# Sparse and stick-breaking attention heads taken in pairs, in a fused block kernel on one core

## The reference, cut to what matters

```python
# even layer: 8 query heads of 64, 2 key/value heads, indexer of 4 heads, 64 keys kept per query
q, k, v, qi, ki, wi, u = split(h @ w_in)                 # q and k are RMS-normed per head
score = (relu(qi @ ki.T) * wi).sum(heads) * IDX_SCALE    # causal
_, sel = top_k(score, 64)
attn = softmax(q @ k[sel].T * 64 ** -0.5) @ v[sel]
pooled = multiscale_pool(u) @ pool_w * pool_scale        # 4 groups of 128
x = x + concat([attn, pooled]) @ w_out                   # 1024 x 1024
# odd layer: 16 heads of 64
z = q @ k.T * 64 ** -0.5
brk = where(s < t, softplus(z), 0)
a = where(s < t, exp(log_sigmoid(z) - sum_of_later(brk)), 0)
x = x + (a @ v) @ w_out
```

## Time and profile before

| what | value |
|---|---|
| three runs | 1335.97, 1337.49, 1373.87 us; median 1337.49 |
| profiled execution | 1334.04 us, its span 1332.3 us |
| mean granted clock of PE in it | 0.977 of full speed |
| busy: PE, DVE, ACT, POOL | 1245.0 (93%), 785.6 (59%), 613.4 (46%), 107.6 us (8%) |
| DMA moved | 219.94 MB, 164 GB/s read |

### The profile page before, as it was taken

How to read it: one execution, slowest core, us unless ns; L and a number is a source line. 1 busy time by engine, 2 the same in 40 slices (tenths; PEclk the granted TensorE clock), 3 DMA queues, 4 the chain that set the end, 5 groups by cost and what they waited for, 6 DMA issues and landing times.

```text
span 1332.3 us, 21042 instructions
## 1 busy us (share of the span) xinstructions
PE 1245.0 (93%) x8609; PEld 1139.1 (85%) x8609; DVE 785.6 (59%) x1245; ACT 613.4 (46%) x950; POOL 107.6 (8%) x172
## 2 busy tenths in 40 slices
PE   2899999998989899999998699999999999899998
PEld 2889989876789899887888479999989887899997
DVE  7888987654595354555546756555554433655554
ACT  2557623433455354554444335434453654544442
POOL 0200000031030000112100410000000133000000
PEclk9999999999999999999989589999999999999999
DMA  9896779402557465322522054555545322555552
GB/s 328 293 307 190 253 249 313 165 1 85 184 175 215 124 213 165 124 91 69 170 92 72 32 177 141 190 189 189 190 158 171 114 96 76 176 173 183 186 189 95
DMA packets 164880, 219.94 MB, mean 165 GB/s; under 512 B 5868, under 2 KB 135696, under 8 KB 164784
## 3 DMA queue, kind: packets, MB, share of 16 engines
q1 hardware_dynamic: 163984, 216.82, 50.3%
q0 software_dynamic: 800, 1.77, 0.4%
HBM read 217.53 MB, written 1.05 MB: 164 GB/s over the span
## 4 chain that ended last, share of the span: by engine, by line
PE 74%; DVE 12%; DMA 6%; ACT 6%; issue 2%; SPq 0%; ACTq 0%; DVEq 0%
PE ps L646 12%; PE ps L650 11%; PE ps L647 11%; PE ps L709 5%; PE ps L714 5%; PE ps L710 5%; DMA raw_weights<-in_a_w_in 4%; DVE w_lo L1592 4%; PE ps L687 3%; PE ps L682 3%; PE ps L683 3%; DVE acc L1674 2%; ACT w_hi L1271 1%; PE ps L962 1%; PE ps L907 1%
## 5 line engine op out<-in xcount | busy, mean ns | idle before, releaser
L1592 DVE TENSOR_TENSOR w_lo<-raw_weights,w_hi 128x1024 fp32r<-128x1024 f32 x348 | 423.7, 1228 | 282.3 <-ACT w_hi L1271 280.7
L1271 ACT ACTIVATE w_hi<-raw_weights 128x1024 fp32r<-128x1024 f32 x348 | 362.8, 1054 | 415.5 <-PE ps L714 110.6
L646 PE MATMUL ps<-act_hi,w_hi 128*128 128x256 f32 x1616 | 405.6, 289 | 3.8 <-ACT w_hi L1271 3.8
L647 PE MATMUL ps<-act_lo,w_hi 128*128 128x256 f32 x1616 | 397.4, 283 | 0.0
L646 PEld LDWEIGHTS ps<-act_hi,w_hi 128*128 128x128 f32 x1616 | 310.4, 192 | 12.1 <-issue 8.5
L647 PEld LDWEIGHTS ps<-act_lo,w_hi 128*128 128x128 f32 x1616 | 310.7, 192 | 3.3 <-issue 2.4
L650 PE MATMUL ps<-act_hi,w_lo 128*128 128x256 f32 x1616 | 228.0, 284 | 7.1 <-DVE w_lo L1592 7.1
L650 PEld LDWEIGHTS ps<-act_hi,w_lo 128*128 128x128 f32 x1616 | 209.2, 193 | 8.0 <-DVE w_lo L1592 7.9
L709 PE MATMUL ps<-w_hi,act_hi 128*128 128x512 f32 x320 | 126.7, 396 | 2.5 <-DVE work L1777 1.9
L710 PE MATMUL ps<-w_hi,act_lo 128*128 128x512 f32 x320 | 125.4, 392 | 0.0
L714 PE MATMUL ps<-w_lo,act_hi 128*128 128x512 f32 x320 | 86.9, 392 | 0.0
(11 more groups left out here) (258 smaller groups left out, 1421.4 us busy)
## 6 DMA issues: line engine op xcount, KB each, us to landing
raw_weights<-in_ffn_w SPq DMA_DIRECT2D x66, 1024.0 KB, 5.2
raw_weights<-in_a_w_in SPq DMA_DIRECT2D x32, 1024.0 KB, 6.1
raw_weights<-in_mod_w SPq DMA_DIRECT2D x24, 1024.0 KB, 5.9
raw_weights<-in_kv_w SPq DMA_DIRECT2D x16, 1024.0 KB, 5.6
raw_weights<-in_b_w_in SPq DMA_DIRECT2D x16, 1024.0 KB, 5.4
raw_weights<-in_od_w_qkv SPq DMA_DIRECT2D x12, 1024.0 KB, 5.2
raw_weights<-in_kv_mod_w SPq DMA_DIRECT2D x8, 1024.0 KB, 5.8
raw_weights<-in_a_w_out SPq DMA_DIRECT2D x8, 1024.0 KB, 5.0
```

What stands on the lines that cost most here:

```text
L646: pe.matmul(dst, wh[:, k, :], act_hi[:, base + k, :], start=(k == 0), stop=False)
L647: pe.matmul(dst, wh[:, k, :], act_lo[:, base + k, :], start=False, stop=False)
L1271: act.activation(half_view(w_hi, s), HALVES[s][2], ACT.Copy).then_inc(hi_done, 1)
L1592: dve.tensor_tensor(half_view(w_lo, s), HALVES[s][2], half_view(w_hi, s).bitcast(F32), ALU.subtract).then_inc(lo_done, 1)
```

## The change

- **Sparse section, order of weights:** `ev_u`, `ev_q`, `ev_kv` in place of `ev_kv`, `ev_q`, `ev_u`; output chunks pooled first (4, 5, 6, 7, then 0 to 3). The pooling matmuls come before the heads, the scale of the pooled result moves from DVE to ACT.
- **Sparse section, heads:** four pairs instead of eight single heads. Two heads' matmuls stand one behind the other on different halves of the array's rows (logits) or columns (values) and in different PSUM banks. The output chunks stand between the steps of the pairs. ACT, not DVE, copies the outputs. DVE's splits stand at other rounds of the selection.
- **Stick-breaking section:** eight pairs in ten steps with two halves each. DVE writes the breaks twice, as fp32 and rounded to fp32r; POOL subtracts the two; the break matmuls run on both parts as fp32r, 6 per head instead of 3 of fp32. The two `affine_select` per head go; an fp32r matmul of the identity by a matrix with a large negative number adds the mask to z.
- **Constants:** the identity's 128 KB come by POOL's queue instead of SP's; the masks come as two transfers.
- **Banks:** the even layer's output sum moves to banks 0 to 3, which the projections use.

```diff
@@ -64,9 +64,9 @@
             pieces.append(("mod", *mods.pop(0)))
     pieces += [("forget", 0)] + [("b_in", n) for n in (*range(8, 16), *range(8))]
     pieces += [("b_out", n) for n in range(8)]
-    pieces += [("ev_qi", 0), ("ev_small", 0), ("ev_kv", 0), ("ev_q", 0), ("ev_q", 1), ("ev_u", 0), ("ev_u", 1),
+    pieces += [("ev_qi", 0), ("ev_small", 0), ("ev_u", 0), ("ev_u", 1), ("ev_q", 0), ("ev_q", 1), ("ev_kv", 0),
                ("pool_w", 0)]
-    pieces += [("ev_out", n) for n in range(4)]
+    pieces += [("ev_out", n) for n in (2, 3, 0, 1)]
...
@@ -103,11 +103,12 @@
     add("q", "v" * 8)
     add("norm2", "vvvv")
     add("ev_i", "aa")
+    add("ev_u", "aa")
+    add("ev_q0", "v")
+    add("ev_q1", "v")
     add("ev_k", "v")
     add("ev_v", "a")
-    add("ev_q", "vv")
-    add("ev_u", "aa")
-    add("ev_pool", "vv")
+    add("ev_pool", "aa")
     add("norm3", "vvvv")
     add("up0", "v" * FC)
...
@@ -216,7 +223,7 @@
 
         def y_bank(j, t, n):
 
-            return ps[:, (0 if j in (1, 4) else 4) + 2 * t + n, :]
+            return ps[:, (0 if j in (1, 2, 4) else 4) + 2 * t + n, :]
...
@@ -489,6 +507,7 @@
 
         @block.gpsimd
         def _(pool):
...
+            pool.wait_ge(st("ds_split"), HE // 2)
+            pool.tensor_scalar(far_r, causal[:, 0:P], -1.0, FAR, ALU.is_ge, ALU.mult).then_inc(st("sb_far"), 1)
+            for p in range(HO // 2 + 2):
+                if p < HO // 2:
+                    for h in (2 * p, 2 * p + 1):
+                        pool.wait_ge(st("sb_soft"), h + 1)
+                        pool.tensor_tensor(sb_brk_lo[h % 2], sb_brk[h % 2], sb_brk_hi[h % 2].bitcast(F32), ALU.subtract)\
+                            .then_inc(st("sb_lo"), 1)
+                if 1 <= p <= HO // 2:
+                    c = p - 1
                     split_output(c, o_full[:, c % 2, :], st("sb_out"), st("sb_split"), OUT2 + c)
 
         down_half = {}
...
+                for t in range(NT):
+                    for e, rows in enumerate(pair_rows):
+                        ins = pe.matmul(ds_bank(p, e)[:, P * t:P * t + P * (t + 1)], evq[rows, p, t * P:(t + 1) * P],
+                                        evk[rows, p // 2, 0:P * (t + 1)], start=True, stop=True)
+                ins.then_inc(st("ds_logits"), 1)
+
+            def ds_turn(p):
+                pe.wait_ge(st("ds_prob"), p + 1)
+                for e in range(2):
+                    for b in range(3):
+                        blk = slice(b * P, (b + 1) * P)
+                        ins = pe.transpose(ds_bank(p, e)[:, blk], ds_prob[:, p % 2, e, blk], ident)
+                ins.then_inc(st("ds_turned"), 1)
+
...
+                for e, rows in enumerate(pair_rows):
+                    pe.matmul(ds_bank(p, e)[rows, 0:T], v[0], ds_probT[:, e, 0:T], start=True, stop=False)
+                for e, rows in enumerate(pair_rows):
+                    ins = pe.matmul(ds_bank(p, e)[rows, P:T], v[1], ds_probT[:, e, T:S3], start=False, stop=True)
+                ins.then_inc(st("ds_o"), 1)
+
+            def ev_out_chunk(c):
+                if c == 4:
+                    pe.wait_ge(unit_free["a"], before("a", unit[0] - 1))
+                    pe.wait_ge(unit_free["v"], before("v", unit[0] - 1))
+                if c >= 4:
+                    pe.wait_ge(st("ev_pooled"), (c - 4) // 2 + 1)
+                else:
+                    pe.wait_ge(st("ds_split"), c + 1)
+                out_half("ev_out", OUT2 + c, c == 4, c == 3)
...
+            ds_logits(0)
+            ev_out_chunk(4)
+            ds_logits(1)
+            ev_out_chunk(5)
+            ds_turn(0)
+            ev_out_chunk(6)
+            ds_pv(0)
+            ds_turn(1)
+            ds_logits(2)
+            ev_out_chunk(7)
+            ds_pv(1)
+            ds_logits(3)
+            ev_out_chunk(0)
+            ds_turn(2)
+            ev_out_chunk(1)
+            ds_pv(2)
+            ds_turn(3)
+            ev_out_chunk(2)
+            ds_pv(3)
+            ev_out_chunk(3)
...
+                for bank, _ in pair:
+                    pe.matmul(diagonal_blocks(bank[:, 0:S3]), ident_r,
+                              far_r.rearrange("p (b t) -> p b t", b=1).to_broadcast([P, 2, P]),
+                              start=True, stop=False, skip_group_check=True)
+                for bank, rows in pair:
+                    pe.matmul(bank[:, 0:T], odk[rows, p, 0:P], odq[rows, p, :], start=False, stop=False,
+                              skip_group_check=True)
+                for bank, rows in pair:
+                    ins = pe.matmul(bank[:, T:S3], odk[rows, p, P:T], odq[rows, p, P:T], start=False, stop=False,
+                                    skip_group_check=True)
+                ins.then_inc(st("sb_z"), 1)
+
+            def minus_breaks(p):
+
+                for h in (2 * p, 2 * p + 1):
+                    bank = sb_bank(h)
+                    pe.wait_ge(st("sb_lo"), h + 1)
+                    for b in (sb_brk_hi[h % 2], sb_brk_lo[h % 2]):
+                        pe.matmul(bank[:, 0:T], neg_after_r, b[:, 0:T], start=False, stop=False, skip_group_check=True)
+                        pe.matmul(bank[:, P:T], neg_ones_r, b[:, T:S3], start=False, stop=False, skip_group_check=True)
+                        ins = pe.matmul(bank[:, T:S3], neg_after_r, b[:, T:S3], start=False,
+                                        stop=(b is sb_brk_lo[h % 2]), skip_group_check=True)
+                    ins.then_inc(st("sb_log"), 1)
...
+            pe.wait_ge(x_done, 16)
+            pe.wait_ge(st("sb_far"), 1)
+            od_bank = [None]
+            for p in range(HO // 2 + 2):
+                if p >= 2:
+                    weighted_values(p - 2)
+                dense_half(2 * p)
+                if 1 <= p <= HO // 2:
+                    minus_breaks(p - 1)
+                if p < HO // 2:
+                    z_scores(p)
+                dense_half(2 * p + 1)
             pe.wait_ge(st("sb_split"), 8)
             out_half("od_out", OUT2 + 7, False, True)
...
+            ds_exps(0)
+            advance(first_out + 3)
+            ds_exps(1)
+            advance(first_out + 4)
+            ds_take_turned(0)
+            advance(first_out + 5)
+            ds_take_out(0)
+            ds_take_turned(1)
+            advance(first_out + 6)
+            ds_exps(2)
+            ds_take_out(1)
+            advance(first_out + 7)
+            ds_exps(3)
+            ds_take_turned(2)
+            ds_take_out(2)
+            ds_take_turned(3)
+            ds_take_out(3)
...
+            last_v = unit_half[FIRST["od_v"] + 3]
+            for p in range(HO // 2 + 1):
...
+                advance(last_v + NSPLIT + 2 * p - 1)
+                if p >= 1:
+                    for h in (2 * p - 2, 2 * p - 1):
+                        act.wait_ge(st("sb_log"), h + 1)
+                        if p >= 2:
+                            act.wait_ge(st("sb_o"), p - 1)
+                        act.activation(sb_prob[h % 2], sb_bank(h)[:, 0:S3], ACT.Exp).then_inc(st("sb_exp"), 1)
...
+                        if p >= 1:
+                            act.wait_ge(st("sb_soft"), h - 1)
+                        link(act.activation(sb_ln_t[e], sb_bank(h)[:, 0:S3], ACT.Abs))
+                        link(act.activation(sb_ln_t[e], sb_ln_t[e], ACT.Exp, scale=-1.0))
+                        act.activation(sb_ln_t[e], sb_ln_t[e], ACT.Ln, bias=1.0).then_inc(st("sb_ln"), 1)
+                    advance(last_v + NSPLIT + 2 * p)
...
+            def choose(q, n, splits):
...
                 for r in range(TOPK // 8):
-                    if r % 4 == 2:
-                        advance(ahead + r // 4)
+                    if r in splits:
+                        advance(splits[r])
...
+            choose(Q1, T, {0: last_i + 4, 2: last_i + 5, 4: last_i + 6, 6: last_i + 7, 8: last_i + 8})
+            normed("ev_q0", 0, 16, evq[:, 0:2, :], ev_q_gain)
+            choose(Q0, P, {2: last_i + 9, 5: last_i + 10, 8: last_i + 11})
+            normed("ev_q1", 0, 17, evq[:, 2:4, :], ev_q_gain)
+            normed("ev_k", 0, 18, evk, ev_gain[:, 1:2])
+            first_out = first_half[AT[("ev_out", 2)]]
+            split_pooled(0)
+            ds_maxima(0)
+            advance(first_out + 3)
+            ds_scales(0)
+            split_pooled(1)
+            ds_maxima(1)
+            advance(first_out + 4)
+            ds_scales(1)
+            advance(first_out + 5)
+            ds_maxima(2)
+            advance(first_out + 6)
+            ds_scales(2)
+            ds_maxima(3)
+            advance(first_out + 7)
+            ds_scales(3)
...
+                if p >= 2:
+                    c = p - 2
+                    dve.wait_ge(st("sb_o"), c + 1)
+                    if c >= 2:
+                        dve.wait_ge(st("sb_split"), c - 1)
+                    dve.tensor_copy(o_full[0:HD2, c % 2, :], sb_bank(2 * c)[0:HD2, 0:T])
```

(47 more changed lines are left out.)

338 lines of the change are left out of this document (127 added, 211 removed).

## The result

The changed kernel took 1317.82 to 1323.47 us in four runs, median 1321.94; the four runs of before beside it 1335.97 to 1373.87. The ratio is **0.9878**, with the 95% interval 0.9842 to 0.9913: faster by 1.2%, some 16 us, which is less than the 2% set for "faster". The forecast was 1309, with a range of 1297 to 1325. So the direction and the range were right, and the saving of its sum, 25.9 us, was 1.6 times the 16 measured. The profiled execution took 1323.47 us, its span is 1321.7.

The account below looks back on a forecast made before the run. The prediction took the kernel as bound by PE, with the sparse section also bound by one head's chain and the clock. Sparse −15.6, clock +2 and stick-breaking −12.3 gave −25.9 on 1334.0, so 1309 us, range 1297 to 1325.

Parts of the forecast that it names:

- PE's work in the pairs: Both sections: a sparse pair takes 3.4 us of PE; a stick-breaking step takes 9.55, 1.6 less than two rounds.
- The second rival: Logits, z and values of both sections: the pairs don't share the array, giving 1323 us; chance 0.10.
- The waits of the sparse section: Sparse section: PE's new waits, for splits, first logits and the pairs' chains, 13.5 us together, bounds 0 and 21.
- I expect one short drop: +2: Sparse section: with chunks between pairs the granted clock drops once briefly, costing 2 us.
- The first rival: Sparse section, from near 722 to the norm: the clock stays down, +36 instead of +2, 1343 us; chance 0.10.
- The text's own sign of being wrong: Sparse section: a clock at 0.5 for more than 10 us behind 722 would show the forecast wrong.
- the 71.8 of the sum: Sparse section from the indexer's end: PE work without waits, 34.5 projections, 1.6 pooling, 22.1 chunks, 13.6 heads.
- the added subtraction and the second DVE write lie beside the two halves: Stick-breaking section: POOL's and DVE's added work hides behind PE's two halves, slack at least 0.5; section saves 12.3 us.
- The text's lower bound: Stick-breaking section: saving of only 3.4 us if z and values do not share the array at all.
- The third rival: Stick-breaking section: POOL's subtraction comes late, breaks 1.5 us late per pair, +12, 1321 us; chance 0.12.
- The end of the sum: Whole kernel: −25.9 on the profiled 1334.0 gives 1308.1; undisturbed runs lie 1.9 and 3.5 above that execution; so 1309.
- the main case: Whole kernel: no rival happens, 1301 to 1316 us, chance 0.56, of which about 0.34 lies below 1310.7.

Follow-up runs that it names:

- e7: The changed kernel with a pair's logits, z and values matmuls ordered head by head, z's mask matmul between the heads; ratio 0.9943.
- e4: The changed kernel with the two last splits in the lower queries' selection behind rounds 2 and 3 instead of 5 and 8; 1312.70 us, ratio 0.9821.
- e5: The changed kernel with DVE copying the stick-breaking key units ahead of its late splits instead of behind them; 1308.68 and 1310.87 us, ratio 0.9806.
- e11: The changed kernel itself, run again beside the other kernels on their chip; median 1318.09 us, ratio 0.9868.
- e12: The changed kernel with the edits of e4 and e5 together, run again beside the changed kernel; 1302.74 us, ratio 0.9756.
- e10: The kernel of e12 plus five fp32 matmuls of constants that nothing reads, just ahead of the first logits; ratio 0.9763.
- e9: The kernel of e12 with the key norm's square sum on PE and scale on ACT ahead of the pooling; ratio 0.9775.
- e8: The changed kernel with breaks as fp32 matmuls, without DVE's second write and POOL's subtraction; 1318.46 us, ratio 0.9871.

## Why the prediction was right in direction and wrong in size

- **PE's work in the pairs: right, and better than forecast.** A step of 9.39 (9.55 forecast): breaks 1.32 (1.4), mask 0.37 (0.24), z 0.86 (0.95), values 0.80 (1.0). In the sparse section six transposes take 0.57 ahead of a chunk and 0.80 ahead of logits (1.4), values 0.80. The second rival is refuted by e7. The rule that the text weighed with it, that a weight load overlaps matmuls in flight only for other rows (the Trainium skill, "TensorE: Matmul & The Clock Gate", The mechanism), is not what decides here: two heads on the same rows and different columns take 0.80, as long as one.
- **The waits of the sparse section: right in sum.** Forecast 13.5; the brackets give 1.40 + 1.77 + 2.29 + 1.40 + 0.78 + 0.87, and 1.33 + 2.15 for POOL's split ahead of the last two attention chunks, 12.0.
- **The clock in the sparse section: the step that failed there.** "PE is idle for at most 2.6 at a time, and I expect one short drop: +2" was too low by 8: e4, which removes nothing but two waits, has 8 us less of busy time behind the indexer, 6.5 of them right behind these waits. The first rival had the mechanism, its place near 722 to 732, and a chance of 0.10; it came true for just under a third of its length (about 733 to 747, then for 3 us of 750 to 755 and 3 from 788 on). The text's own sign of being wrong, 0.5 for more than 10 us behind 722, was there.
  - Other terms set off part. PE's work at full clock was 2.4 less than the 71.8 of the sum, by cheaper heads (an estimate: e4's 71.2 busy us behind the indexer, less 1.8 for its own short drop at 738 to 742), the waits 1.5 less, and the norm's wait 1.3 less: 8 − 5.2 leaves the 2.6 that are missing behind the indexer; the other 1.7 lie ahead of it. That the error of 8 shows as so little is luck.
  - The earlier trace rows had a warning, but not the one that I took from it. PE ran 687.5 to 694.0 fully busy at 0.51, and in the trace of before this stretch doesn't stand behind a wait:

```profile
674.18:687.50 13.32, 13.32 (x114) 13.32 (x115) 7.21 (x11) 5.84 (x10) 0.00 (x0) 1.00 0.32 91
```

PE had been busy without a break for 13.3 us, the last 4.6 of them with matmuls of 4 columns, when the clock fell. All the kernels here have a low stretch at this place. So a fully busy PE can stay at the lower level for 6.5 us, for which a "short drop" of +2 left no room. I had read it as a trait of the norm.
- **The stick-breaking section: the step that failed there** is "the added subtraction and the second DVE write lie beside the two halves", with the section held to be bound by PE alone. That was so before (100.72 of 101.30), and it stopped being so at one place: the first output chunk needs the banks of the last keys, and DVE, with two splits per step instead of one between its writes, copies them 4 us late. e5 undoes this and gives 7.3 (6.0 beside e11): 3.1 of idle, 2.4 of the chunk at 1.2 GHz and 0.6 of other busy time, 1.2 for the waits of 0.6. With it the second interval is 323.5, and the forecast's 336.5 − 12.3 = 324.2 is met. (The text's lower bound, −3.4 if z and values share nothing, should be 12.3 − 10.6 = −1.7 by its own terms; nothing hangs on it.) I had followed the order of the changed rows and not asked what the helper in front of the copy does first.
- **The third rival** (POOL's subtraction late) didn't happen: no wait of PE in the section names it. POOL's subtraction takes 1.01 alone and 1.95 beside a DVE split (1072.45), as the earlier trace rows led one to expect and as the Trainium skill, "SBUF — State Buffer", Who interferes with whom, has it; the slack covered it.
- **The end of the sum:** 1308.1 and undisturbed runs 1.9 and 3.5 above give 1310 to 1311.6, not 1309. With that the main case leans less to "faster", which had 0.50 against 0.48 for "the same" and didn't come.
- **Constants and start:** no effect stands out of the noise; the first mark varies by up to 23 us among kernels with the same code ahead of it (666.72 in e12, 690.00 in e5); for e5 the trace shows the clock as the reason.

With both failed steps repaired the kernel runs at 1302.7, 6 below the forecast: the second interval is 0.6 above its forecast (324.8 against 324.2), the first 6.7 below (110.4 against 117.1), by the cheaper heads and the waits for splits, 0.24 instead of the 3.6 put in.

## What to carry to other kernels

When a change moves work between engines, go through the stream of the engine that gets it, and find the first place where the bound engine waits for a buffer that this stream frees; helpers that do work ahead belong to that stream. Price a wait of PE at more than its length: here 3.2 us of waits cost 9.4, and 4.1 us cost 5.5 to 6.6, while a wait that was filled or shortened (e10, e9, one trace each) only moved the low clock to the next one. So remove waits in a row together, as e4 did. That those with solid work behind them should go first is my inference and wasn't tested against another order.

## What the runs showed of the hardware

- Two waits of 1.40 and 1.77 us, 1.2 us apart, were followed by 10 to 14 us of the 1.2 GHz level with PE busy throughout (L1078 at 0.21 a matmul), in all seven kernels that have them; without them the same work ran at 1.00, in all five.
- The length of one wait doesn't settle it: waits of 2.13 to 2.15 ahead of the last chunk were followed by a stretch at 0.50 in six kernels and by 1.00 in six others. And the level fell with no wait at all in the 13.3 us before (687.5 in the trace of before).
- In e10 PE work that nothing reads stood in the wait for the first logits, and the clock stayed at 1.00 there (one execution).
- Matmuls of two heads on two halves of the array's rows or columns and in different banks cost as much as those of one head: z 0.86 for two, 0.85 for one; values 0.80 and 0.79. With a full-array matmul between them two z take 0.84 + 0.85.
- fp32 transposes in a row start 0.11 apart (six in 0.57 ahead of a chunk), half of what an fp32 matmul of 128 columns takes (0.22 in e8): a matmul's time is no guide for a transpose's.
- Left open: why the untouched stretch at 250 to 300 us ran at 0.56 in one execution of e5 and at 1.00 in that of the changed kernel. It moves the marks behind it by some 18 us, more than the whole change gains.
